# Two transformer blocks on one Trainium2 core: the first query tile's normalisation in halves, and differential attention with its turns, rotations and value products in another order

## The reference

```python
def swiglu(h, w_gate, w_up, w_down):
    return (jax.nn.silu(h @ w_gate) * (h @ w_up)) @ w_down

def diff_mixer(h, w_in, w_out, lam, subln_g, cos, sin, layer_idx):
    proj = h @ w_in
    q = apply_rope(proj[..., :B_QK].reshape(B, S, 2, B_HEADS, B_HEAD_DIM), cos, sin)
    k = apply_rope(proj[..., B_QK:2 * B_QK].reshape(B, S, 2, B_HEADS, B_HEAD_DIM), cos, sin)
    v = proj[..., 2 * B_QK:].reshape(B, S, B_HEADS, B_V_DIM)
    ...
        s = jnp.einsum('btchd,bschd->bchts', q_b, k32) * scale
        p = jax.nn.softmax(s, axis=-1)
        a = p[:, 0] - lam_val * p[:, 1]
        o = jnp.einsum('bhts,bshe->bthe', a, v32)
        o = rmsnorm(o, subln_g) * (1.0 - lam_init)
    ...
# each sublayer: x = x + gate * rmsnorm(sublayer(modulate(rmsnorm(x, g), shift, scale)), post_g)
```

## Time and profile before

| | us |
|---|---|
| three timed executions | 2032.58, 2038.41, 2036.50 |
| their median | 2036.5 |
| the profiled execution, its own time | 2034.79 |
| its span in the profile | 2033.0 |
| mean granted clock of TensorE | 0.973 |

### The profile page before, as it was taken

How to read it: one execution, slowest core, us unless ns; L and a number is a source line. 1 busy time by engine, 2 the same in 40 slices (tenths; PEclk the granted TensorE clock), 3 DMA queues, 4 the chain that set the end, 5 groups by cost and what they waited for, 6 DMA issues and landing times.

```text
span 2033.0 us, 30145 instructions
## 1 busy us (share of the span) xinstructions
PE 1913.7 (94%) x12007; PEld 1646.7 (81%) x12007; DVE 1396.7 (69%) x1877; ACT 974.6 (48%) x1377; POOL 80.4 (4%) x173
## 2 busy tenths in 40 slices
PE   8999999989899999997999978999999999789998
PEld 7988687878588888876999864899989989648997
DVE  3873444536799889897788684588768875746754
ACT  4664402223577777764333545434444345564432
POOL 6000000000000000000000000000000000000000
PEclk9999999979899999998999989999999999899999
DMA  8443432126999999994897521599579957136652
GB/s 259 148 147 123 145 104 83 43 102 222 390 330 346 349 324 340 367 345 136 302 321 260 192 83 42 202 323 326 175 255 324 324 176 235 44 111 213 215 186 103
DMA packets 214398, 442.84 MB, mean 218 GB/s; under 512 B 8780, under 2 KB 159590, under 8 KB 196880
## 3 DMA queue, kind: packets, MB, share of 16 engines
q1 hardware_dynamic: 207728, 424.70, 60.2%
q0 software_dynamic: 6560, 16.63, 2.4%
HBM read 440.16 MB, written 1.14 MB: 217 GB/s over the span
## 4 chain that ended last, share of the span: by engine, by line
PE 69%; DVE 6%; ACT 5%; issue 1%; DMA 1%; SPq 0%; ACTq 0%; DVEq 0%
PE P L803 68%; ACT merged L1740 1%; DVE w_lo L2347 1%; ACT w_hi L1772 1%; DVE h L2300 1%; ACT sparse_slot L1740 1%; DVE xs L2300 1%; PE P L1415 0%; ACT proj L1740 0%; ACT st L1740 0%; DMA ring<-in_w_down 0%; DMA ring<-in_w_gate 0%; DVE merged L2293 0%; DVE h L3036 0%; DVE st L3034 0%
## 5 line engine op out<-in xcount | busy, mean ns | idle before, releaser
L803 PE MATMUL P<-x_parts,w_hi 128*128 128x256 f32 x2560 | 459.7, 282 | 2.6 <-DVE w_lo L2347 2.6
L803 PEld LDWEIGHTS P<-x_parts,w_hi 128*128 128x128 f32 x2560 | 396.0, 188 | 14.1 <-DVE w_lo L2347 4.6
L2347 DVE TENSOR_TENSOR w_lo<-ring,w_hi 128x1024 fp32r<-128x1024 f32 x302 | 351.9, 1220 | 74.1 <-ACT w_hi L1772 73.9
L803 PE MATMUL P<-w_hi,x_parts 128*128 128x256 f32 (+2 forms) x1504 | 375.5, 336 | 7.3 <-DVE w_lo L2788 4.4
L803 PE MATMUL P<-x_parts,w_lo 128*128 128x256 f32 x1280 | 359.5, 281 | 0.0
L1772 ACT ACTIVATE w_hi<-ring 128x1024 fp32r<-128x1024 f32 x302 | 299.0, 1051 | 85.0 <-DMA ring<-in_ffn_w_down 60.3
L2788 DVE TENSOR_TENSOR w_lo<-ring,w_hi 128x1024 fp32r<-128x1024 f32 x240 | 280.7, 1221 | 29.9 <-ACT w_hi L2010 27.3
L803 PEld LDWEIGHTS P<-w_hi,x_parts 128*128 128x128 f32 x1504 | 259.5, 192 | 42.8 <-issue 11.0
L2010 ACT ACTIVATE w_hi<-ring 128x1024 fp32r<-128x1024 f32 x240 | 240.9, 1052 | 87.5 <-DMA ring<-in_w_up 32.6
L803 PEld LDWEIGHTS P<-x_parts,w_lo 128*128 128x128 f32 x1280 | 241.1, 188 | 0.0
L803 PE MATMUL P<-w_lo,x_parts 128*128 128x256 f32 (+2 forms) x752 | 235.3, 334 | 0.0
(11 more groups left out here) (507 smaller groups left out, 2718.6 us busy)
## 6 DMA issues: line engine op xcount, KB each, us to landing
mod_w<-in_ada_w SPq DMA_DIRECT2D x52, 1024.0 KB, 10.1
ring<-in_ffn_w_gate SPq DMA_DIRECT2D x44, 1024.0 KB, 5.5
ring<-in_ffn_w_up SPq DMA_DIRECT2D x44, 1024.0 KB, 10.0
ring<-in_ffn_w_down SPq DMA_DIRECT2D x44, 1024.0 KB, 5.0
ring<-in_w_in SPq DMA_DIRECT2D x40, 1024.0 KB, 5.7
ring<-in_w_gate SPq DMA_DIRECT2D x40, 1024.0 KB, 4.9
ring<-in_w_up SPq DMA_DIRECT2D x40, 1024.0 KB, 5.0
ring<-in_w_down SPq DMA_DIRECT2D x40, 1024.0 KB, 5.2
```

The lines of the kernel that those rows point to most:

```text
L803: return pe.matmul(o, l, r, start=start, stop=stop, **kw)
L2347: dve.tensor_tensor(w_lo[:, slot, c:c + half], ring[:, slot, c:c + half], w_hi[:, slot, c:c + half].bitcast(F32), ALU.subtract).then_inc(s ...
```

## The change

**Halves in the turnover.** For tile 0, `residual` (but not behind the last sublayer) writes `xs` in two halves of 512 columns and tells `row` behind each; ACT squares each half by itself (`row_squares_halves`: two squares, with a scaling of the first sum between them, instead of one square); `pre_norm(0)` writes `h` in two halves, and PE waits for the first half before its first four products and for the second before the other four. Behind the experts only `pre_norm(0)` is in halves. Tile 1 is as it was.

**A down product moved.** In the last pass of `four_tiles` the third down product (group 2) is formed for tile 0 alone; its part for tile 1 (six products of 512 columns) stands behind the two last gate and up products, at the head of tile 1's part. For this the last pass is written out behind the loop, which has one pass less.

**Differential attention.** The queries are rotated as soon as their eight steps are out; they are turned behind steps 12 and 13, into `rowbc` instead of a slot of `w_hi`. The first half of the keys is rotated behind the low parts of units 8 and 9; the second half, for each tile by itself, behind everything that stood ahead of `masked_rows(0)`. The keys of tile 0 are turned behind `values(0)`, those of tile 1 behind `scores(0)`. `values(1)` stands ahead of `scores(1)`, and in the loop `values(n + 2)` stands where `values(n + 1)` stood. The two buffers of the probabilities change places.

```diff
@@ PE, turn_normed
-                t.see("turnable")
                 for b in range(2):
+                    if b == 0 or i == 0:
+                        t.see("turnable")
@@ PE, four_tiles
-                    x = down(g, 128, wd, g % 2, r * 4 + (h0 + g + 1), start=False, stop=False)
+                    x = down(g, 128, wd, g % 2, r * 4 + (h0 + g + 1), start=False, stop=False, tiles=last_down if f == 3 else (0, 1))
@@ PE, ffn
-                with pe.Fori(chunks % 4, 4) as r:
+                with pe.Fori(chunks % 4, 3) as r:
                     four_tiles(n0 + 6, r, h0 + 4)
...
+                four_tiles(n0 + 6, 3, h0 + 4, (0,))
...
                 for i in range(2):
+                    if i:
+                        down(2, 128, held, 0, k0 - 1, False, False, (i,))
                     x = down(3, 128, held, 1, k0, False, False, (i,))
@@ PE, differential
                 for n in range(16):
                     project_step(sub, DIFF_COLS, n)
+                    if n == 12:
+                        t.see("roped")
+                    if n in (12, 13):
+                        turn_heads(n - 12, 0)
...
                 values(0)
                 t.see("roped")
-                for i in range(2):
-                    turns([proj[:, i, 128 * k:128 * k + 128] for k in range(16)])
+                turn_heads(0, D)
                 pe.wait_ge(sem("turned"), t.sent["turn"])
...
                 scores(0)
+                t.see("roped")
+                turn_heads(1, D)
+                values(1)
                 scores(1)
+                pe.wait_ge(sem("turned"), t.sent["turn"])
                 for n, (i, hg) in enumerate(units):
                     if n + 2 < len(units):
                         scores(n + 2)
-                    if n + 1 < len(units):
-                        values(n + 1)
+                    if n + 2 < len(units):
+                        values(n + 2)
@@ ACT, row_squares_halves (called for tile 0 in turnover)
+                one, two = st[:, 12 + i:13 + i], st[:, 14 + i:15 + i]
+                a.see("row")
+                f(acc[:, i, 0:512], xs[:, i, 0:512], ACT.Square, accum_out=one)
+                f(one, one, ACT.Identity, scale=1 / D, bias=eps_ln[:, 1:2])
+                a.see("row")
+                f(acc[:, i, 512:D], xs[:, i, 512:D], ACT.Square, accum_out=two)
+                f(st[:, 8 + i:9 + i], two, ACT.Sqrt, "row_rs", scale=1 / D, bias=one)
@@ ACT, a_differential
-                a_project(n)
+                a_project(n, {12: lambda: head_columns(0, qT_d), 13: lambda: head_columns(1, qT_d)})
...
                 softmax_exps(0, 0, bigs_d)
+                values_out(1)
@@ DVE, pre_norm
-                stt(h[:, i, :], xs[:, i, :], st[:, 8 + i:9 + i], pre_scale, ALU.mult, ALU.mult, "turnable")
+                for c in (slice(0, D),) if i else (slice(0, 512), slice(512, D)):
+                    stt(h[:, i, c], xs[:, i, c], st[:, 8 + i:9 + i], pre_scale[:, c], ALU.mult, ALU.mult, "turnable")
@@ DVE, v_differential
-                low(unit[0], range(2, 10))
-                dve.wait_ge(sem("proj_out"), proj_before[0] + 16)
+                low(unit[0], range(2, 8))
+                dve.wait_ge(sem("proj_out"), proj_before[0] + 8)
                 for i in range(2):
-                    apply_rope(i, 0, 32)
+                    apply_rope(i, 0, 16)
                 v.mark("roped")
+                low(unit[0], (8, 9))
+                dve.wait_ge(sem("proj_out"), proj_before[0] + 12)
+                for i in range(2):
+                    apply_rope(i, D, 8)
                 low(unit[0], (10, 11))
...
                 copy(hid[:, 0, 128:256], causal_neg[:, :])
+                for i in range(2):
+                    dve.wait_ge(sem("proj_out"), proj_before[0] + 15 + i)
+                    apply_rope(i, D + 512, 8)
+                    v.mark("roped")
```

31 lines of the change are left out of this document (20 added, 11 removed).

## The result

| | median us | executions |
|---|---|---|
| kernel before, on the same chip | 2035.97 | 2032.51 to 2043.46 (10) |
| changed kernel | 2025.51 | 2021.68 to 2033.96 (10) |
| ratio | 0.9946 | 95% interval 0.993 to 0.9962 |

The change takes 10.5 us off, over twice the 5.0 us of the forecast, and the time lies just under the lower end of the range. A second set, on another chip, gave 0.9953 (0.9934 to 0.9973). The profiled execution took 2025.82 us, with a span of 2024.1 us against 2033.0: 8.9 us less.

The account below looks back on a forecast made before the run. PE, busy 94% of the span, was taken as the bound, through its waits and low clock. Turnovers −4.8, clock −3.0 and differential attention +2.8 made −5.0 us: 2031.5 us from a median of 2036.5, range 2026 to 2039.

Parts of the forecast that it names:

- Which part gives the gain: Whole kernel: turnovers −4.8 us, the clock behind them −3.0, differential attention +2.8, the unrolled pass nothing.
- The moved product: Ffn turnovers: six products go behind `out` of tile 0, which comes 1.4 us sooner behind ffn 0, 2 and 3.
- Rival 4: Ffn turnovers: ACT or DVE take `out` no sooner despite the moved product; −1.1 us, 2035.4; chance 0.07.
- The halves: Turnovers: halved residual and square lose 0.05 us; halved `pre_norm` takes 0.5 us off PE's wait, costs DVE 0.26 us.
- I take 3 us: Behind ffn 0 and 2: gain from the low clock vanishing as PE's waits shrink, taken below the most possible.
- the 4.1 us put as the most: Clock behind the ffns: low stretches cost 2.9 us behind ffn 0 and 1.2 us behind ffn 2, together the upper limit.
- three equal waits with two outcomes: Waits of 2.13 us behind ffn 0, 2 and 3: low clock after two, none after ffn 3; used to discount the clock gain.
- Rival 1: Both clock drops behind the ffns vanish and `values(1)` runs at full clock: −7.5 us, 2029.0; chance 0.28.
- Differential attention, +2.8 us: Its new order starts the loop 2.8 us later (1.4 to 5.5), with PE waiting ten us for the keys' rotation.
- 4.1 was put, 5.5 the bound: Differential attention: scores 1 come 4.1 us later than before (3.4 to 5.5).
- Nothing comes back: Differential attention's loop: the value product missing in the seventh round was hidden anyway, so none of the delay is regained.
- What was to be seen: Signs: wait behind ffn 3 0.2 to 0.6 us, full clock behind ffn 0 and 2, a nine-to-eleven-us rotation wait, scores 1 later.

Follow-up runs that it names:

- down_only: Kernel before with only the down product moved (last pass written out): 2023.3 us, ratio 0.9941 to the kernel before.
- no_row_halves: Changed kernel with residual and square of a turnover's first tile whole again, the norm's halves kept: 2024.93 us, ratio 0.9945 to the kernel before.
- unroll_only: Kernel before with the last pass of the ffn loop written out, no product moved: 2033.7 us, ratio 1.0004.
- down_again: Kernel before with only the down product moved, run once more beside the filled waits: 2025.21 us, ratio 0.9955 to the kernel before.
- turnovers: Changed kernel with differential attention as before, so halves and moved down product alone: 2023.12 us, ratio 0.9944 to the kernel before.
- diff_only: Kernel before with the new order of differential attention alone: 2034.56 us, ratio 1.0004.
- fill_two: Kernel before with two full 128-row products filling the wait for h behind ffn 0, 2 and 3, nothing moved: 2031.41 us, ratio 0.9989.
- gains_first: Changed kernel with gains and mask moved into DVE's idle time ahead of low parts 10 and 11: 2025.78 us, ratio 0.996 to the kernel before.

## Why the prediction fell short

- **Which part gives the gain** was right: the moved product and the clock behind it, not the halves nor differential attention. The kernel's gain is that of `down_only`.
- **The moved product**, 1.4 us at each ffn: right. 2.13 us became 0.73 in `down_only`, and `out` of tile 0 had moved. Rival 4 fell.
- **The halves**: right in sum. ACT's square pair was 2.13 us (2.05 put). The halved norm alone took 0.54 us off PE's wait, as put: 0.73 us in `down_only`, 0.19 in `no_row_halves`, and 1.18 and 0.64 behind the attentions. The halved residual and square gave 0.13 us of it back (0.33 and 0.77 in the changed kernel), where 0.05 was put. Behind an ffn the new wait of 0.50 us for DVE's columns, put at 0.4, took the rest.
- **"I take 3 us" for the clock**: this is the step that failed. Between the first traces PE's busy time in B fell by 4.4 us for the same products. Behind ffn 0 the clock was worth 2.9 us and behind ffn 2 1.4: from turn to fifth step 20.29 and 18.47 us before became 17.42 and 17.04 in `down_only` (18.20 and 17.83 in the changed kernel, with the new waits of 0.50 and 0.20 us in them). So the 4.1 us put as the most was reached in full. Taken over three traces each (before twice and `unroll_only`; `down_only`, `down_again` and `turnovers`) B fell from 539.7 to 531.9 us; 2.8 of the 7.8 are the two shorter waits in it, 5 are left for the clock, sparse attention's share in it. The reason for the discount was wrong: from three equal waits with two outcomes I concluded that the fall would partly stay or be missing anyway. The kernels with the product in its old place are low in 12 of 15 places, those with it moved in none of 33: the chance lies within the old state, not in whether the new one escapes it. A smaller slip is in the cost as well: the earlier trace rows make the low window behind ffn 2 half as long as that behind ffn 0, not 40%. Rival 1 had the right mechanism behind the ffns.
- **Differential attention, +2.8 us**: the chain was right and the sum was not. The wait was 10.38 us and the rotation 1.5 us, as put. Scores 1 came 5.3 us later, 1.8 us by the sixteen transposes and 3.5 us from the start of the 16th step on (22.54 us became 26.02); 4.1 was put, 5.5 the bound. Up to `square_out` the order cost 4.8 us between the first traces and 3.8 between the means of the traces of either order (127.6 and 123.8). "Nothing comes back" failed: `square_out` gives back 3.0 us by its clock, so that C is 1.8 us longer between the first traces and 0.9 by the means. That `diff_only` shows no change in the total (1.0004) agrees.
- **The sum, redone**: between the first traces the shorter waits in A and B gave 5.0 us (4.8 was put for all turnovers), the clock in B 4.4 (3 put), and C took 1.8 (2.8 put). The other 1.3 us, 0.3 up to the experts and 1.0 in their part of A, lie in unchanged code and are chance: 8.9 us, where 5.0 was forecast. The other 1.5 us of the median's 10.5 is the draw of the profiled executions. So about half of the miss is the clock and differential attention, and the other half luck. The time missed the range by 0.5 us; the second set's 2026.13 lies just inside it.
- **What was to be seen**: 0.33 us behind ffn 3 (0.2 to 0.6), clock 1.00 behind ffn 0 and 2, one wait of 10.38 us (nine to eleven), no shorter seventh round: all came, so behind the ffns the mechanism was read rightly and its price was not. The return in `square_out` was in none of the signs.

## What to carry to other kernels

A wait of TensorE can cost what it lasts and what a low clock takes behind it. Here moving 1.4 us of real products into a gap of 2.8 us was worth 9 to 12 us over three places (the ratios of `down_again` and `down_only`), of which 4.2 us are the waits themselves; filling the gap with idle products was not shown to be worth anything in the total (`fill_two`: 2.2 us, −0.2 to 4.9). One trace shows one draw of the clock: where an argument rests on a low stretch, take a second trace of the same kernel; here it had three of three places low instead of two. When an order is changed, put the work that is waited for ahead of the work that merely fits: here the rotation of 1.5 us ahead of the last low parts, with the gains in DVE's idle time and ACT's drains moved up, was worth 9.3 us of the stage. Moving the gains alone (`gains_first`) took 3.6 us off the wait.
